# A chain of two transformer blocks on one core: full-height spreads, query sums inside two projections, gated outputs around halves of one

## The reference

```python
# first block, attention half: the fused input projection
proj = n @ w_in[layer]                       # 17 tiles of 128 output features
c_q, c_kv, k_rope, dq, dk, dv = jnp.split(proj, IN_SPLITS, axis=-1)
# 8 heads of 96 features: q and k are RMS-normed per head; 4 x 2 maps of 64 features: the same
y = x * lax.rsqrt(jnp.mean(x * x, axis=-1, keepdims=True) + EPS)
# second block: gated linear attention in 4 chunks of 64 tokens, 4 heads
o = o_intra + o_inter                        # A @ v  +  qd @ S_prev
y_gla = rmsnorm(o, gla_norm_g) * jax.nn.silu(g_o)
```

## Time and profile before

| | us |
|---|---|
| median of 3 runs | 1476.8 |
| lowest and highest | 1476.69 and 1476.99 |
| profiled execution | 1476.6 |
| its span, from first to last instruction | 1474.8 |
| PE busy | 1435.1 |
| VectorE busy | 1000.0 |
| ScalarE busy | 683.8 |
| GpSimd busy | 541.3 |
| mean granted clock of TensorE, of 1 | 0.987 |

### The profile page before, as it was taken

One profiled execution on the slowest core, in us unless ns is written; L12 is line 12 of the kernel. 1 busy time (PEld: TensorE's weight loads), 2 busy tenths in 40 slices (PEclk: granted clock), 3 DMA queues, 4 the chain that ended last, 5 costly groups with the idle time before them and its releaser, 6 DMA issues.

```text
span 1474.8 us, 31771 instructions
## 1 busy us (share of the span) xinstructions
PE 1435.1 (97%) x11218; PEld 1362.6 (92%) x11218; DVE 1000.0 (68%) x2085; ACT 683.8 (46%) x1035; POOL 541.3 (37%) x252
## 2 busy tenths in 40 slices
PE   7999999999999999999999999999999998999997
PEld 6787678999999999999999999999989977899997
DVE  4524454889788888876766666666555754699987
ACT  4432554445555555543333333444454355645553
POOL 3313237778500000024444444444423334354541
PEclk9988999999999999999999999999999999999999
DMA  7410125667755555567777777555543513255552
GB/s 282 136 67 30 43 86 187 191 191 207 232 178 174 178 172 173 175 197 231 233 230 235 228 233 218 189 181 185 184 169 116 175 53 126 88 188 187 180 182 74
DMA packets 89995, 250.17 MB, mean 170 GB/s; under 512 B 10048, under 2 KB 35920, under 8 KB 89296
## 3 DMA queue, kind: packets, MB, share of 16 engines
q1 hardware_dynamic: 86112, 238.20, 51.0%
q10 hardware_dynamic: 3824, 11.17, 2.0%
HBM read 234.09 MB, written 15.24 MB: 169 GB/s over the span
## 4 chain that ended last, share of the span: by engine, by line
PE 92%; DVE 5%; ACT 2%; issue 1%; DMA 0%; ACTq 0%; POOL 0%; DVEq 0%
PE ps L1656 47%; PE ps L2052 28%; PE ps L2035 4%; PE ps L1928 2%; PE ps L1882 2%; PE ps L1671 1%; PE ps L1852 1%; PE ps L1902 1%; DVE big L1074 1%; DVE w_lo L1052 1%; PE ps L1704 1%; PE ps L1741 1%; PE ps L2008 0%; PE ps L1772 0%; DVE big L1066 0%
## 5 line engine op out<-in xcount | busy, mean ns | idle before, releaser
L497 POOL TENSOR_TENSOR w_lo<-raw,w_hi 128x1024 fp32r<-128x1024 f32 x193 | 488.8, 2534 | 806.1 <-ACT w_hi L598 805.9
L1656 PE MATMUL ps<-x_op,w_hi 128*128 128x256 f32 (+1 forms) x3968 | 744.4, 289 | 7.8 <-DVE x_op L1083 2.6
L1656 PEld LDWEIGHTS ps<-x_op,w_hi 128*128 128x128 f32 x3968 | 624.2, 193 | 20.4 <-issue 10.9
L1656 PE MATMUL ps<-x_op,w_lo 128*128 128x256 f32 (+1 forms) x1984 | 566.1, 285 | 0.0
L598 ACT ACTIVATE w_hi<-raw 128x1024 fp32r<-128x1024 f32 x400 | 420.4, 1055 | 266.2 <-PE ps L2052 214.3
L2052 PE MATMUL ps<-h_op,w_hi 128*128 128x256 f32 x2400 | 426.8, 280 | 2.4 <-DVE h_op L1606 2.4
L1656 PEld LDWEIGHTS ps<-x_op,w_lo 128*128 128x128 f32 x1984 | 383.5, 193 | 0.0
L2052 PEld LDWEIGHTS ps<-h_op,w_hi 128*128 128x128 f32 x2400 | 368.1, 188 | 3.1 <-issue 1.8
L1052 DVE TENSOR_TENSOR w_lo<-raw,w_hi 128x1024 fp32r<-128x1024 f32 x207 | 265.1, 1281 | 120.6 <-ACT w_hi L598 120.4
L2052 PE MATMUL ps<-h_op,w_lo 128*128 128x256 f32 x1200 | 337.7, 281 | 0.0
L2052 PEld LDWEIGHTS ps<-h_op,w_lo 128*128 128x128 f32 x1200 | 225.3, 188 | 0.0
(11 more groups left out here) (270 smaller groups left out, 1062.7 us busy)
## 6 DMA issues: line engine op xcount, KB each, us to landing
raw<-blocks SPq DMA_DIRECT2D x404, 512.0 KB, 3.6
early_store<-kv_mem SPq DMA_DIRECT2D x96, 128.0 KB, 1.7
work<-early_store SPq DMA_DIRECT2D x96, 128.0 KB, 3.4
big<-consts ACTq DMA_DIRECT2D x2, 1336.0 KB, 6.9
big<-h_t ACTq DMA_DIRECT2D x4, 272.0 KB, 3.8
big<-bias_lines ACTq DMA_DIRECT2D x8, 136.0 KB, 2.7
bias_lines<-route_t ACTq DMA_DIRECT2D x4, 264.0 KB, 2.5
res<-mem_t SPq DMA_DIRECT2D x1, 1024.0 KB, 9.6
```

Of the source, the lines that this page charges most:

```text
L497: pool.tensor_tensor(w_lo[:, s, :], raw[:, s, :], w_hi[:, s, :].bitcast(F32), ALU.subtract).then_inc(sem("lo_pool"), 1)
L1656: mm = pe.matmul(ps[:, m_bank, 0:T], w, x, start=(k == 0 and j == 0), stop=(k == last and j == 2))
```

## The change

1. `head_of`, `map_of` and `rk` get 128 rows instead of 8. GpSimd sets them to zero at the start; rows 0 to 7 are written and read by the others as before. The spreads now multiply with 128 rows, 120 of them zeros.
2. The query sums go from bank 2 to columns 480 to 511 of bank 7. The sums over 96 features (two per step) stand behind each of the 8 feature tiles of projection 12, the sums of the maps (one per step) behind those of projection 13. PE waits for `q_root` ahead of the first key spread, since that writes bank 7. The wait for `qk_turned_read` (bank 2) goes to the sum of the lambdas.
3. In the second block, the first half of projection 10 stands between the gated outputs of `f` = 0 and those of `f` = 1, the second half behind them.

```diff
-        head_of = area(HEADS * QK, rows=HEADS)
-        map_of = area(2 * DH * 64, rows=2 * DH)
+        head_of = area(HEADS * QK)
+        map_of = area(2 * DH * 64)
-        rk = area(2, NK, rows=8)
+        rk = area(2, NK)
-        sub_r = rk[:, 0, 0:NQ]
+        sub_r = rk[0:8, 0, 0:NQ]
+        q_sums = 512 - 32
             pool.memset(pair_in, 0.0)
+            pool.memset(head_of, 0.0)
+            pool.memset(map_of, 0.0)
+            pool.memset(flat2(rk), 0.0)
...
             for w, e in enumerate((E_QK, E_64)):
-                ins = act.activation(rq[:, w].rearrange("p t h -> p (t h)"), ps[:, 2, 16 * w:16 * w + 16], ACT.Sqrt, bias=e)
+                at = q_sums + 16 * w
+                ins = act.activation(rq[:, w].rearrange("p t h -> p (t h)"), ps[:, 7, at:at + 16], ACT.Sqrt, bias=e)
...
-            def project_in(j):
-                projections(B_IN + j, M_IN + j, 1, NK, operand(R_ATTN) if j == 0 else None)
+            def project_in(j, tiles=range(KT)):
+                n, m = B_IN + j, M_IN + j
+                project(At(n), m % 2, NK, bank_free(m), operand(R_ATTN) if j == 0 else None, tiles)
...
-            project_in(12)
-
-            pe.wait_ge(sem("qk_turned_read"), 2)
-            pe.wait_ge(sem("bank_free"), M_IN + 9)
-            for t in range(2):
-                for h in range(HEADS):
-                    a = h * NQ + P * t
-                    pe.matmul(ps[:, 2, 8 * t + h:8 * t + h + 1], xf[0:QK, a:a + P], ones[0:QK, 0:1], start=True, stop=True)
-                for h in range(DH):
-                    a = 16 + 8 * t + 2 * h
-                    mm = pe.matmul(ps[:, 2, a:a + 2], dq_sq[:, h, P * t:P * t + P], two_in[:, 6:8], start=True, stop=True)
+            for k in range(KT):
+                project_in(12, range(k, k + 1))
+                for t in range(2):
+                    at = q_sums + 8 * t + k
+                    pe.matmul(ps[:, 7, at:at + 1], xf[0:QK, k * NQ + P * t:k * NQ + P * t + P], ones[0:QK, 0:1], start=True, stop=True)
+            for k in range(KT):
+                project_in(13, range(k, k + 1))
+                t, h = k // DH, k % DH
+                at = q_sums + 16 + 8 * t + 2 * h
+                mm = pe.matmul(ps[:, 7, at:at + 2], dq_sq[:, h, P * t:P * t + P], two_in[:, 6:8], start=True, stop=True)
             mm.then_inc(sem("q_sum"), 1)
-            project_in(13)
+            pe.wait_ge(sem("q_root"), 1)
             pe.wait_ge(sem("heads_set"), 1)
...
             pe.wait_ge(sem("lam_ready"), 1)
-            pe.wait_ge(sem("q_root"), 1)
+            pe.wait_ge(sem("qk_turned_read"), 2)
...
-                pe.matmul(ps[:, 2 + h, 0:NQ], map_of[:, P * h:P * h + P], sub_r, start=True, stop=True).then_inc(sem("sub_spread"), 1)
+                pe.matmul(ps[:, 2 + h, 0:NQ], map_of[:, P * h:P * h + P], rk[:, 0, 0:NQ], start=True, stop=True).then_inc(sem("sub_spread"), 1)
...
             for f in range(2):
+                if f:
+                    project(At(B_IN2 + 10), (M_IN2 + 10) % 2, NQ, bank_free(M_IN2 + 10), None, range(KT // 2))
                 for n in range(NCH):
...
             mm.then_inc(sem("gla_out"), 1)
-            project_in2(10)
+            project(At(B_IN2 + 10), (M_IN2 + 10) % 2, NQ, None, None, range(KT // 2, KT))
```

More of the change, by code:

```diff
@@ L749, in _ @@
             act.wait_ge(sem("k_sum"), 1)
-            act.activation(rk[:, 0, :], ps[0:8, 3, 0:NK], ACT.Sqrt, scale=1.0 / QK, bias=E_MODEL[0:8]).then_inc(sem("k_root"), 1)
+            act.activation(rk[0:8, 0, :], ps[0:8, 3, 0:NK], ACT.Sqrt, scale=1.0 / QK, bias=E_MODEL[0:8]).then_inc(sem("k_root"), 1)
             evacuate_in(12)
@@ L758, in _ @@
             act.wait_ge(sem("k_sum"), 2)
-            act.activation(rk[:, 1, :], ps[0:8, 3, 0:NK], ACT.Sqrt, scale=1.0 / 64, bias=E_MODEL[0:8]).then_inc(sem("k_root"), 1)
+            act.activation(rk[0:8, 1, :], ps[0:8, 3, 0:NK], ACT.Sqrt, scale=1.0 / 64, bias=E_MODEL[0:8]).then_inc(sem("k_root"), 1)
             evacuate_in(14)
@@ L1110, in _ @@
             for a, n in ((head_of, QK), (map_of, 64)):
-                ins = dve.tensor_copy(a.rearrange("p (h n) -> p h n", h=8), ident[0:8, 0:8].unsqueeze(2).to_broadcast([8, 8, n]))
+                ins = dve.tensor_copy(a[0:8].rearrange("p (h n) -> p h n", h=8), ident[0:8, 0:8].unsqueeze(2).to_broadcast([8, 8, n]))
             ins.then_inc(sem("heads_set"), 1)
@@ L1160, in _ @@
             dve.wait_ge(sem("k_root"), 1)
-            dve.reciprocal(rk[:, 0, :], rk[:, 0, :]).then_inc(sem("k_inverse"), 1)
+            dve.reciprocal(rk[0:8, 0, :], rk[0:8, 0, :]).then_inc(sem("k_inverse"), 1)
             rq_flat = rq.rearrange("p w t h -> p (w t h)")
@@ L1177, in _ @@
             dve.wait_ge(sem("k_root"), 2)
-            dve.reciprocal(rk[:, 1, :], rk[:, 1, :]).then_inc(sem("k_inverse"), 1)
+            dve.reciprocal(rk[0:8, 1, :], rk[0:8, 1, :]).then_inc(sem("k_inverse"), 1)
             los(B_IN + 16)
```

## The result

Over ten executions each, the changed kernel has a median of 1467.92 us (1465.43 to 1471.82) and the kernel before one of 1476.89 (1474.92 to 1479.97). The ratio is 0.9945, with an interval of 0.9932 to 0.9957. It is faster by 9.0 us in the medians and by 8.2 ± 1.9 in the means; 11.9 were forecast.

A forecast was written before the change was run, and what follows sets the result against it. PE, busy for 97% of the span, was taken as the bound. 5.1 - 0.7 + 3.05 + 0.75 + 2.9 + 0.8 = 11.9 us off the 1476.8 median gave 1464.9; own range 1463 to 1467.5, with rivals 1462.8 to 1471.0.

The forecast's parts named there:

- The mechanism: Across PE's stream: rows and streamed columns count for the granted clock, output width does not; forecast chance 0.63.
- rival 1: At the full-height spreads: rows of zeros do not hold the clock, 3.05 us stay lost, 1468.0 us; chance 0.14.
- rival 2: The clock falls inside projections 12 and 13 with their inserted sums: 1470.8 us, or 1466.6 if it recovers; chance 0.14.
- An inserted tile: In projection 12: three matmuls of a tile at 0.38 us plus four passes of sums at 0.42.
- The new wait: Behind projection 13, PE waits for `q_root` before the first key spread: 0.7 us lost, between 0.4 and 1.1.
- The change of shape: Around 8-row spreads: each change of array shape costs 0.19 us; four go, 0.76 us gained, at worst 0, at best 1.0.
- Spreads and gated outputs: Full-height spreads gain 3.05 us by clock and 0.75 by shape; gated outputs around halves of projection 10 gain 2.9.
- VectorE's key scaling: Between second key spread and map spread: projection 15 at 3.02 us still covers it; cost nothing, at worst 0.4 us.
- the query sums: From projection 12 to the first key spread: 16.34 us become 11.27 with sums between matmuls, a gain of 5.07.
- Behind: At the cross attention's warm-up near 1238 us: less half clock, between nothing and 1.7 us gained, 0.8 taken.
- Rival 3: Slower: the clock falls at the attention entry and stays low to the third memory block, 18.5 us lost, 1483.4; chance 0.03.
- Rival 4: Half the gain turns into waits for VectorE, ScalarE or the loads: 1470.8 us; chance 0.06.

The follow-up runs named there:

- the upper group of the sums alone: Kernel before with only the query sums moved inside projections 12 and 13: the seven of twelve executions between 1476.9 and 1478.9 us.
- the kernel with 8 rows: Kernel before with each of the two key spreads run five times over, operands of 8 rows: 1507.53 us in one execution.

## Why the prediction was right, and where its size was off

**The mechanism is right.** In these profiles the clock falls behind matmuls with few rows or few streamed columns though PE never idles, and full height or neighbours of full width keep it. The median is 1467.92 us, inside the range of 1462.8 to 1471.0 but 0.4 us above the forecast's own range of 1463 to 1467.5. It stands next to the 1468.0 of rival 1, which the experiments refute: the time alone would have pointed at the wrong cause, and only the pieces and the parts tell them apart. In the ten profiles with full-height key and map spreads no cold stretch begins behind one; in the four with 8 rows at least one does. In all eight profiles where the sums stand between matmuls of the projections, the clock stays at 1.00 there, so rival 2 was seen in none. It isn't excluded for the upper group of the sums alone, seven executions without a profile. In all six with the sums in one run it falls among them or right behind. Gated outputs in one run end in a fall in all five such profiles, those around half a projection in none of nine. For the height, an experiment changes nothing else; for the few columns and for the gated outputs it is these counts that speak. Heights between 8 rows and full were not tried.

The rule of the Trainium skill behind rival 1 ("TensorE: Matmul & The Clock Gate", section "Why this matters for your kernels") advises against idle gaps between bursts of matmuls. It is not enough here: no gap stands in the 17.10 us at 0.50 of the kernel with 8 rows.

**The prices at full clock are right.** An inserted tile costs 0.82 us where 0.38 + 0.42 = 0.80 was worked out, so projections 12 and 13 with their sums took 11.5 us and not 11.27. The new wait cost a gap of 0.5 us (108.41 to 108.92) and 0.25 at the spread, together 0.75 against 0.7; placed evenly, the sums don't have it. The change of shape at 0.19 us goes where the spreads got 128 rows: 1.83 instead of 2.00, 3.02 instead of 3.2. Spreads and gated outputs measured alone gave 4.2 and 3.0 us, against 3.8 and 2.9, each with 1.3 to 1.7 us of noise. That VectorE's key scaling would just be covered by a projection of 3.02 us is right too: the map spread follows at once, at 121.00.

**The mis-sized term is the query sums: 5.1 less 0.7, so 4.4 forecast; 1.1 ± 1.9 alone, and 2.0 ± 1.4 with the rest in place.** The working took the 16.34 us of one profile as what that stretch costs. Its row is the dearer of two prices: over the six profiles with the sums in one run it is 16.34, 16.31, 13.11, 16.30, 16.16 and 13.12 us, so about 16.3 in four of them, 13.1 in two and 15.2 in the mean, and the stretch with the sums divided as in the changed kernel is 12.0 in all four profiles that have it. That makes 3.2 us, or 1.1 in an execution like the cheap ones. The other one or two microseconds seem to be given back behind it: the stretch ends earlier, and later thin places fall that did not before. Two such returns were seen: 1.5 us behind the sub-norm spread (24.73 instead of 23.25 with the sums alone, and 24.72 with the gated outputs alone, where the sums drew the cheap price), and 2.0 at the attention's entry (in two of these four profiles). No sum over profiles closes this account, since one profile of each kernel is one draw; that share is inferred, and with the rest in place the interval still reaches 3.2 us, by which nothing would be given back.

**"Behind", 0.8 us, was the second error of the same kind.** The warm-up at the cross attention took 4.65, 5.84 and 5.86 us in three profiles of the changed kernel, 5.5 in the mean against 5.63 before. By these few profiles what is gained there is 0.2, not 0.8.

**Rival 3** named the place of the other loss, the attention's entry, and called a short fall there "at most 1.7" us. It came, cost 1.98, and went after 6.8 us; it did not last until the memory blocks. Its long form was priced too low: the 37 us of PE's work up to the third memory block take 37 more at half clock, by the prediction's own rule, and not 18.5. Of rival 1's evidence, line 1704 kept 1.00 only in part: 40 passes from 11.28 us did, while the 30 at 1244.03 stand mostly at 0.50. Rival 4, that VectorE, ScalarE or the loads swallow half, is refuted by the pieces: the gains of the pieces make up the whole gain in span, -11.2 of -11.1.

**The start** had no term. The 0.7 us of the first profile arise in PE's first group, 16 matmuls from 5.79 us: 5.66 us before, 6.35 here, 6.57 and 6.68 in the other two profiles of the changed kernel. The new memsets do not explain it: the four profiles with evenly divided sums have them too, and 5.35 to 5.64 us. The start as a whole moved by 0.7, 3.5 and 3.7 us in the changed kernel's three profiles against the one of before (projection 12 starts at 96.91, 99.70, 99.88 instead of 96.20), and by -0.3 to +0.7 in the others but one. That one, with 2.9, has nothing of the change (8 rows, five times over). So it goes with the execution. Whether the changed kernel draws the slow start more often than the one before stays open: one profile of a kernel is too few, and the times of before don't show it apart.

Against the median the forecast was 3.0 us too low, because it took one profile's cold stretches for what they cost in every execution, and added nothing for new ones. The profiled execution, 11.2 us faster than that of before against 11.9 forecast, agrees better by luck: the dearer price of the sums stood in the profile before, and no fall at the start or the attention's entry in the one after.

## What to carry to other kernels

Where PE is the bound, look for stretches of matmuls with few rows or few columns: give them zero rows up to full height, which costs nothing in the stream (1.83 us instead of 2.00 for eight passes here), or stand them singly between full ones, with the last pieces free of them if somebody waits for the result. Price the cold stretch that goes by its mean over several profiles and not by the one at hand, and allow for a part of it to return at the next thin place. Measure with many executions: here two profiles of the same kernel differ by 6 us. If the times fall into groups, compare the mean granted clock of the executions, and take a profile of each group.

## What the runs showed of the hardware

- Rows of zeros held the clock up: 40 passes of 272 columns with 120 of 128 rows zero took 9.17 us at 1.00, and 15.04 and 13.81 us with 8 rows only, most of it at 0.50.
- Thin work can hold the clock down, not only bring it down. A spread of 8 rows left 3.3 us at half clock behind it; with five times as many the cold stretches lasted 17.1 and 13.7 us, of which 11.4 and 9.2 us were such spreads.
- Which thin place falls differs from execution to execution of the same program: the attention's entry kept 1.00 in one profile of the changed kernel and lost 1.98 us in two.
- The first key spread behind the wait for ScalarE's roots takes 2.08 us, and the same spread without a gap ahead 1.83.
